# A hybrid attention and convolution layer pair on one core: the row pieces of the adaptive gate lead, its last third is summed between the key rotations, and the first convolution block and the attention's gates are loaded in another order

## The reference, cut to what matters

```python
mod = c @ w_ada + b_ada                       # c: 1 x 1024, w_ada: 1024 x 3072
shift, scale, gate = split(mod, 3)
h = rmsnorm(x, norm_g) * (1 + scale) + shift  # x: 1024 x 1024
proj = h @ w_in                               # glu_a, glu_b, z_conv, q, k, v, z_att, g_conv, g_att
u = conv31(glu_a * sigmoid(glu_b)) + conv_b   # depthwise, along the sequence
y_conv = (silu(layernorm(u)) * silu(z_conv)) @ w_conv_out
q, k = rope(q), rope(k)                       # 3 dilation groups x 8 heads of 64
att = combine(window_attention(q, k, v) of the 3 groups by their max and sum)
y_att = (att * silu(z_att)) @ w_att_out
merged = sigmoid(g_conv) * y_conv + sigmoid(g_att) * y_att
x = rmsnorm(x + gate * (merged @ w_o), final_g)
# a second block follows: pooling, sliding window attention, and an MLP of 4096; the change does not touch it
```

## Time and profile before

| | |
|---|---|
| median of 3 runs | 2579.94 us (2577.8 to 2580.2) |
| the profiled execution's own time | 2578.96 us |
| its span, first to last instruction | 2576.8 us |
| PE busy | 2498.2 us, 97% of the span |
| DVE busy | 1555.6 us, 60% |
| ACT busy | 854.0 us, 33% |
| POOL busy | 674.8 us, 26% |
| mean granted clock of PE | 0.993 of full |
| moved by DMA | 300.83 MB, mean 117 GB/s |

### The profile page before, as it was taken

The page is one execution under the profiler, slowest core; times in us unless marked ns, Lnnn a source line. Parts: engine busy times, 40 slices in busy tenths (PEclk is TensorE's granted clock), DMA queues, the critical chain, the costliest instruction groups (busy, mean ns, idle before and its releaser), DMA issues.

```text
span 2576.8 us, 31389 instructions
## 1 busy us (share of the span) xinstructions
PE 2498.2 (97%) x12016; PEld 2052.6 (80%) x12016; DVE 1555.6 (60%) x2476; ACT 854.0 (33%) x1664; POOL 674.8 (26%) x653
## 2 busy tenths in 40 slices
PE   7999999999999999989999999999999999999997
PEld 4787887887888887778888888887887788887876
DVE  7511348978778686565646521123557866858778
ACT  5213221122321232463114033231145545354553
POOL 3422224323244232322533332223310000000000
PEclk9999999999999999999999999999999999999999
DMA  7311212213231232633434122215449575666754
GB/s 254 103 49 46 71 64 61 71 42 99 83 94 48 75 97 77 220 103 131 131 132 140 30 86 74 74 66 176 137 121 294 129 190 154 166 193 163 193 127 105
DMA packets 162794, 300.83 MB, mean 117 GB/s; under 512 B 22098, under 2 KB 46418, under 8 KB 158804
## 3 DMA queue, kind: packets, MB, share of 16 engines
q1 hardware_dynamic: 142724, 250.05, 29.3%
q0 software_dynamic: 18768, 44.57, 9.5%
q10 hardware_dynamic: 1152, 4.19, 0.4%
HBM read 232.50 MB, written 57.87 MB: 113 GB/s over the span
## 4 chain that ended last, share of the span: by engine, by line
PE 79%; DVE 12%; DMA 2%; ACT 2%; issue 2%; POOL 1%; SPq 0%; DVEq 0%; ACTq 0%; POOLq 0%
PE ps L2294 52%; PE ps L2520 19%; DVE scr L1650 5%; PE ps L2418 3%; PE ps L2394 2%; PE ps L2404 2%; PE ps L2323 1%; DVE w_lo L2034 1%; DMA h2c_d<-late_hi 1%; DVE w_lo L2043 1%; DVE big L2092 1%; DMA vreg<-in_w_ada 1%; DVE scr L1630 0%; DVE big L1890 0%; DMA late_hi<-in_w_ada 0%
## 5 line engine op out<-in xcount | busy, mean ns | idle before, releaser
L2294 PE MATMUL ps<-act_hi,w_hi 128*128 128x512 f32 x1344 | 540.0, 402 | 13.5 <-DVE act_lo L1529 4.1
L1067 POOL CAST w_hi<-raw 128x512 fp32r<-128x512 f32 x288 | 216.1, 750 | 1224.4 <-DMA raw<-in_w_in 776.3
L2294 PE MATMUL ps<-act_lo,w_hi 128*128 128x512 f32 x1344 | 534.7, 398 | 0.0
L2294 PE MATMUL ps<-act_hi,w_lo 128*128 128x512 f32 x1344 | 527.1, 392 | 0.0
L1650 DVE SCALAR_TENSOR_TENSOR scr<-scr,small 128x512 f32<-128x512 f32 x480 | 431.9, 900 | 15.6
L1069 POOL TENSOR_TENSOR w_lo<-raw,w_hi 128x512 fp32r<-128x512 f32 x288 | 402.8, 1399 | 23.1
L2294 PE MATMUL ps<-w_hi,act_hi 128*128 128x512 f32 (+1 forms) x960 | 377.2, 393 | 4.3 <-POOL w_lo L1069 2.6
L2294 PE MATMUL ps<-w_hi,act_lo 128*128 128x512 f32 (+1 forms) x960 | 369.9, 385 | 0.0
L2294 PE MATMUL ps<-w_lo,act_hi 128*128 128x512 f32 (+1 forms) x960 | 369.2, 385 | 0.0
L2520 PE MATMUL ps<-w_hi 128*128 128x512 f32 x896 | 350.6, 391 | 10.8 <-issue 7.7
L2520 PE MATMUL ps<-w_hi,w_lo 128*128 128x512 f32 x896 | 349.4, 390 | 0.0
(11 more groups left out here) (235 smaller groups left out, 2682.3 us busy)
## 6 DMA issues: line engine op xcount, KB each, us to landing
raw<-in_w_in SPq DMA_DIRECT2D x176, 256.0 KB, 3.3
late_hi<-h2c_d SPq DMA_DIRECT2D x21, 1024.0 KB, 7.5
vreg<-in_w_ada SPq DMA_DIRECT2D x36, 256.0 KB, 5.3
raw<-in_w_in SPq DMA_DIRECT2D x72, 128.0 KB, 2.4
raw<-in_w_up POOLq DMA_DIRECT2D x8, 1024.0 KB, 12.0
late_lo<-in_w_up SPq DMA_DIRECT2D x8, 1024.0 KB, 5.4
late_lo<-in_w_up POOLq DMA_DIRECT2D x8, 1024.0 KB, 15.8
late_lo<-late_lo POOLq DMA_DIRECT2D x8, 1024.0 KB, 7.4
```

Source lines behind the costliest of these rows:

```text
L1067: pool.tensor_copy(dhi, src).then_inc(w_hi_done, 1)
L2294: ins = nc.tensor.matmul(out_, lhs, rhs, start=(m == 0), stop=(m == 3 * nk - 1))
```

## The change

Four things are reordered.

1. In `ADA` the row pieces (1, k) and (3, k) come before (0, k) and (2, k), with no lag, and PE multiplies them ahead of the turn of the x block with the same k.
2. The gate's 16 sums follow the k rotations instead of the q rotations. SP issues six of the 16 pieces as before, loads the bias row, waits for the rotation tables, and issues the other ten in pairs behind the first five k units, each behind one weight piece. `gate_rows`, the bias and the store move to the third, fifth and seventh v unit; ACT waits for the last sum before it writes the first v block over the buffers, and PE waits for the finished gate row before attention.
3. SP issues the first convolution block's load before the store of the last item of attention 2 instead of after the waits for what attention has stored.
4. The attention's gates are loaded in two halves of 512 positions, the first where the whole was, the second after the loads for the second block.

```diff
@@ -40,9 +40,7 @@
-ROW_LAG = 2
-ADA = ([(n, k - (ROW_LAG if n in (1, 3) else 0)) for k in range(8 + ROW_LAG) for n in (0, 2, 1, 3)
-        if 0 <= k - (ROW_LAG if n in (1, 3) else 0) < 8]
+ADA = ([(n, k) for k in range(8) for n in (1, 3, 0, 2)]
        + [(n, k) for n in (4, 5) for k in range(8)])
@@ -701,10 +699,11 @@
-            for p in range(32, 48):
+            for p in range(32, 38):
                 ada_piece(p)
             sp.wait_ge(ada_col, 3)
             sp.dma_start(mrow, A["b_ada_row"][:, 2 * D:3 * D]).then_inc(gate_b, 16)
+            sp.wait_ge(rope_tab, 2)
@@ -788,6 +794,10 @@
                 w = us[-1]
+                if g == NG - 1:
+                    sp.wait_ge(c_st, 16 * 16)
+                    sp.wait_ge(pv, 16 * NG)
+                    conv_block(0)
                 store_item(w, feature_tile(DST[w[0]], w[1], w[2]))
@@ -797,20 +807,16 @@
                     conv_io(u)
-                    if u == ("k", 0, 6):
+                    if u[:2] == ("k", 0) and u[2] < 5:
+                        ada_piece(38 + 2 * u[2])
+                        ada_piece(39 + 2 * u[2])
+                    if u == ("v", 0, 6):
                         gate_store()
@@ -827,20 +833,22 @@
             prefetch_z(0)
-            sp.wait_ge(c_st, 16 * 16)
...
-            sp.wait_ge(pv, 16 * NG)
-            conv_block(0)
...
-            sp.dma_start(attzT, gate_d["za"].rearrange("(k p) s -> p k s", p=P)).then_inc(za_ld, 16)
+            def za_load(h):
+                cols = slice(HALF * h, HALF * h + HALF)
+                sp.dma_start(attzT[:, :, cols], gate_d["za"].rearrange("(k p) s -> p k s", p=P)[:, :, cols]
+                             ).then_inc((za_ld, za2_ld)[h], 16)
+
+            za_load(0)
@@ -853,6 +861,8 @@
                     attention_rest(u[1] + 1)
+                    if u[1] == 0:
+                        za_load(1)
@@ -1176,6 +1186,8 @@
+                    if B == 0 and g == 0:
+                        act.wait_ge(ada_used, ADA_SUM[(5, 7)])
                     copy_unit(u, V[:, B, :])
@@ -1714,10 +1726,10 @@
-                    if u[:2] == ("q", 0):
+                    if u[:2] == ("k", 0):
                         for p in (32 + 2 * u[2], 33 + 2 * u[2]):
                             ada_sum(*ADA[p])
-                    if u == ("k", 0, 4):
+                    if u == ("v", 0, 4):
                         dve.wait_ge(gate_mm, 1)
@@ -1793,7 +1805,7 @@
-                dve.wait_ge(za_ld, 16)
+                dve.wait_ge((za_ld, za2_ld)[B // 4], 16)
@@ -2349,17 +2361,13 @@
             for B in range(NB):
+                for n in (1, 3):
+                    mod_piece(n, B)
                 pe.wait_ge(x_norm, B + 1)
                 for h in range(2):
                     turn(("xt", B, h), [xs[B % XS][:, P * i:P * i + P] for i in range(4 * h, 4 * h + 4)])
-                if B >= ROW_LAG:
-                    for n in (1, 3):
-                        mod_piece(n, B - ROW_LAG)
             mod_cols(0, ps_s[0])
             mod_cols(2, ps_s[0])
-            for k in range(NB - ROW_LAG, KT):
-                for n in (1, 3):
-                    mod_piece(n, k)
@@ -2446,9 +2454,11 @@
-                    if u == ("k", 0, 2):
+                    if u == ("v", 0, 2):
                         gate_rows()
                 wait_evac(pe, ("v", g, 7))
+                if g == 0:
+                    pe.wait_ge(gate_sum, 2)
                 attention(g)
```

More of the change, by code:

```diff
@@ L369, in build @@
         gate_mm, gate_sum, gate_st = sem("gate_mm"), sem("gate_sum"), sem("gate_st")
-        gs_ready, h_aff = sem("gs_ready"), sem("h_aff")
+        za2_ld, h_aff = sem("za2_ld"), sem("h_aff")
         ang_ready, rope_tab = sem("ang_ready"), sem("rope_tab")
@@ L771, in _, with conv_block @@
                    "g2p": gate_d["g2p"], "g2a": gate_d["g2a"]}
+            def conv_block(B):
+                if B > 0:
+                    wait_unit(sp, ("lt", B - 1, 1))
+                sp.dma_start(cb.rearrange("p (k s) -> p k s", k=KT),
+                             c_d.rearrange("(k p) s -> p k s", p=P)[:, :, P * B:P * B + P]).then_inc(cb_ld, 16)
             def attention_io(g):
@@ L805, in _ @@
                 attention_io(g)
-            def conv_block(B):
-                if B > 0:
-                    wait_unit(sp, ("lt", B - 1, 1))
-                sp.dma_start(cb.rearrange("p (k s) -> p k s", k=KT),
-                             c_d.rearrange("(k p) s -> p k s", p=P)[:, :, P * B:P * B + P]).then_inc(cb_ld, 16)
             def attention_rest(B):
```

## The result

| | before | after |
|---|---|---|
| median, 11 runs each | 2578.31 us (2577.01 to 2581.26) | 2588.48 us (2582.9 to 2590.92) |
| the profiled execution's own time | 2578.96 us | 2584.24 us |
| its span | 2576.8 us | 2582.4 us |

The ratio is 1.0032, 95% interval 1.0025 to 1.004: **slower by 0.32%**, some 8 us (the medians differ by 10.2), where 5.7 us less had been forecast. The sign was wrong, and the time lies outside the range. The times of after look like two groups: four at 2582.9 to 2586.3 and seven at 2588.1 to 2590.9. With 11 times this is a reading and no more, since the gap between the groups (1.8 us) is no wider than one inside the first (2.1 us). The profiled execution is one of the four: it is 5.3 us slower than the profiled execution of before, so it does not show the whole loss.

What follows compares the result with a forecast made beforehand. PE, busy 97% of the span, was taken as the bound, the DMA engines in the opening; -5.1 - 3.9 + 1.6 + 1.7 = -5.7 us gave 2573.3, or 2574.2 us in the median's terms, range 2570.0 to 2579.5.

Steps and rivals of the forecast that it cites:

- Key rotations instead of query rotations: q to k units: k weights arrive and are split before PE needs them, removing 3.68 and 1.43 us, together 5.1 us.
- The ends: k units: gain between nothing, if another wait takes its place, and 5.1 us; 5.1 taken, as splits finish near 91, PE at 96.
- rival (4): k units: DVE becomes the pace, since rotation and two sums beside splits take 6.56 us against PE's 5.91; 2587.4 us, chance 0.05.
- The first convolution block: After attention 2: earlier load removes 2.81 us of waiting and 1.67 of clock, 4.5 us; net 3.9 us gained.
- the 0.6 at the attention block: First attention block, two units on: PE arrives sooner and waits about 0.6 us for DVE's combination; ends 0 and 2.4.
- what is late next: Behind the first convolution block: DVE's combination for the first attention block, gaining only 1.9 of the 4.5 us.
- The gates in halves: Attention's gates: no PE wait of the stage is released, so nothing was taken, between -0.3 and +0.5 us.
- The opening: Opening: later columns delay the first projection by 1.6 us, and the lower clock behind it adds 1.7 us.
- The give-back of 1.4 us: Opening, affine step to first projection: without splits DVE's work runs 1.7 times faster, giving back 1.4 us.
- (2): k units or first convolution block: another wait takes one gain's place; 2578.1 to 2579.3 us, chance 0.17.
- (3): Opening: costs 8 us instead of 3.3, as PE stops at each row piece in order; 2578.9 us, chance 0.08.
- the list of what would show it: Expected profile signs: no w_lo wait near 100, first k split near 73, no first convolution wait, first projection 1 to 2 us later.

Runs made afterwards that it cites:

- lag0: Kernel before with ROW_LAG 0 instead of 2, so row pieces follow their own block's turn, all ahead of the columns: 2585.91 us, ratio 1.0032.
- shift16: Kernel before with 16 dummy transposes on PE ahead of the first attention: 2581.06 us, ratio 1.0007.
- only_conv: Kernel before with only the first convolution block loaded earlier, the gates in one load: 2582.20 us, ratio 1.0010.
- only_open: Kernel before with only the leading row pieces in the opening: 2585.92 us, ratio 1.0020.
- no_gate: The change with the gate's sums put back between the q rotations, all 16 pieces ahead of the k weights: 2584.12 us, ratio 1.0022.
- paced_no_open: The change with k weights loaded only once the fourth q block is rotated, and the opening of before: 2576.26 us, ratio 0.9984.
- paced: The change with SP loading the k weights only once the fourth q block is rotated, not once the rotation tables stand: 2581.47 us, ratio 1.0005.
- no_half: The change with attention's gates in one load again: 2590.16 us, ratio 1.0049.
- no_conv: The change with the first convolution block loaded after attention's stores have landed, as before: 2588.85 us, ratio 1.0043.
- no_open: The change with the opening of before, row pieces lagging by two blocks: 2578.26 us, ratio 1.0000.

## Why the prediction was wrong, step by step

**Key rotations instead of query rotations: -5.1, measured 0.** The gain itself came to the hundredth (3.67 and 1.41 us in the profile, against 3.68 and 1.43). But the 1.43 is a fall of the clock that not every execution has. Six profiles have the order of before in these units; in before and lag0 the two units take 16.9 us, in shift16, only_conv, only_open and no_gate 14.8, against 11.85 in the change. In shift16, whose first k unit starts at 97.07:

```profile
105.97 0.60 PE L2323 MATMUL ps<-ident,scr 128*128 128x128 f32 x4
...
111.89 0.60 PE L2323 MATMUL ps<-ident,scr 128*128 128x128 f32 x4
```

The waits for w_lo cost 3.0 us there, with no slow unit behind them. So the gain is 5.1 us in some executions and 3.0 in others, which may be why paced_no_open won 4.1 us (0.9984) and not the 6.4 of its two gains.

The step that failed is "The ends: nothing, if another wait takes its place, and 5.1. I take 5.1, since five microseconds lie between 91 and 96." The prediction asked there whether the weights would be early enough, not what their splitting would run beside once it was early. The row was in the trace: a rotation beside splits at 3.77 us, against 0.93 alone. The prediction used that row in its rival (4), priced it in the k units only, and gave it 0.05. It decides in the q units, where four rotations are due in a row and PE is only eight microseconds behind the first one (75.17 to 85.02 - 1.73). Paid there: 1.75 us with two rotations ahead of the splits, about 7 with one or none. The paced run shows this, since one wait of SP takes 7 us off the change and the two intervals lie apart.

**The first convolution block: -3.9, measured -1.3 in the change's profile together with the halves, and +2.6 (1.0010) with the gates whole.** The wait, the clock and the 0.6 at the attention block were right: 2.96 + 1.70 gained, then 0.74 back, from the starts of the same operations in the two timelines. The step that failed is what is late next. It looked at DVE only. It was the DMA engines, already 1.0 busy from 1048 us: the second convolution block's load now stood close behind the gates and took 7.0 or 10.9 us to land, where it took 4.3.

**The gates in halves: nothing, measured about -4 with the earlier block (no_half 1.0049, the change 1.0032; 3.75 us of the stage in the profiles), and some 3 us lost without it (no_conv's profile).** "No PE wait of the stage is released by it" was read from the trace of before, where it is true. With the other edit made, the second convolution block's load queues behind the 2 MB and PE waits 4.51 us. Two edits that were priced apart belonged together. The halves have their own price, the waits for w_lo behind the second half, up to 2.6 us with what follows in the change. no_half has only five runs and each stage time is from one execution, so the 4 and the 3 are rough; the waits themselves are in the rows.

**The opening: +3.3, measured +5.2 to +5.4.** The mechanism was right, both sizes were too small. The affine step started at 45.80, not 44.9, since DVE's constants (43.69 to 45.55), which before ran ahead of the columns, now stood behind the last sums. The give-back of 1.4 us was only half there: 4.05 us from the affine step to the projection, where I had 3.4. So +3.1, not +1.6. The clock cost 2.4 us, not 1.7, as PE idled 4.97 us and stayed at 1.2 GHz from 46 until past 54. In three other profiles with this opening (no_gate, no_conv, only_open) the lower clock comes back between 56 and 60 us, and PE is 6.4 to 6.7 us behind before when it reaches the turn of the first q block, not 5.6.

**Added up.** Along three kernels, by their ratios: 4.1 us won by the gate's third, the block and the halves where the splits come late enough (paced_no_open), 5.4 lost by the opening (paced), 7.0 lost by the collision (the change), together the 8 us lost. Without the leading row pieces the collision costs 4.1 (paced_no_open to no_open); the 3 us between the two are not clear of noise.

**The rivals.** (2) and (3) each hold a half of what happened, (4) names the mechanism at the wrong place. In the list of what would show it, the wait of PE in the q units was missing, and it is the one that told most.

## What to carry to other kernels

When a transfer is brought forward, ask what the work that it releases will run beside, not only whether it comes in time: here POOL's splits slowed DVE fourfold just when PE was waiting for four short DVE steps in a row. An earlier load should be tied to the event that makes it harmless (here the fourth rotation), not to the one that makes it possible. A gain that rests on a fall of the clock should be read in more than one profile: the 1.43 us of the k units stood in two of six. Two edits that use the same queue should be priced together, not one by one. And where the times of a kernel fall into two groups, look for two engines whose order is left to chance, and profile an execution of the slower group before explaining the faster one.

## What was not expected of the hardware

- A short DVE instruction beside POOL takes as long as the POOL instruction that it runs beside: the 128x128 product of a rotation goes from 0.29 to 1.40 us and the 128x64 one from 0.23 to 1.27 beside a w_lo of 1.29, the second 128x128 product from 0.28 to 0.69 beside a cast of 0.61 to 0.68. A 128x512 sum goes from 0.82 to 1.40, so the long one loses little and the short one most. A rotation of four instructions then takes as long as two splits, 3.8 us. The Trainium skill (GPSIMD Engine Reference, 1. Specifications) says that GpSimd shares its SBUF interfaces with VectorE, with contention where an instruction of VectorE has two SBUF inputs. These rows agree.
- The same stretch of the same order of work can have either clock. From 52 to 56 us the granted clock was 1.00 in the profile of before and of no_open, and in shift16, which is the same program up to there, it was 0.57. PE had waited 1.61 us before the first projection in before and 1.48 in shift16. In paced_no_open, after 1.15 us, it was 0.61:

```profile
52.00:56.00 4.00, 4.00 (x13) 3.15 (x12) 3.60 (x5) 2.31 (x3) 0.00 (x0) 0.61 0.01 1
```

- That fall moves PE by about 1.5 us (1.48 in paced_no_open and 1.56 in shift16 at the turn of the first q block) but not the rope tables or the loads tied to them, and so changes how many rotations are over when the splits begin. It is the likely source of the two groups; that link was seen in single profiles and not tested by itself.
- A full set of DMA engines alone does not make a load late. In before, a 512 KB load took 4.3 us to land with the engines' share at 1.02, issued 8.4 us behind the 2 MB of the gates. Issued 3.4 us behind 1 MB of them in the change it took 7.0 us, and 3.4 us behind 2 MB in no_half 10.9 us.
